# D of the RWKV inverse from the transposed E, and the GLA output's products grouped by shape

## The reference

```python
# RWKV-7, per token (8 heads of 64)
S = S * d - (S @ kk)[..., None] * (kk * a) + v[..., None] * k
y = S @ r
# GLA, per chunk of 32 tokens (4 heads, key 64, value 128)
att = where(causal, qe @ (k * exp(-b)).T, 0)
o = att @ v + qe @ S
S = S * exp(b_end) + (k * exp(b_end - b)).T @ v
```

## Time and profile before

| | before |
|---|---|
| median of 3 runs | 2339.72 us (2336.74 to 2341.12) |
| the profiled execution | 2343.12 us, its span 2341.3 us |
| PE busy | 2105.8 us, 90% of the span |
| DVE busy | 661.2 us, 28% |
| ACT busy | 343.9 us, 15% |
| mean granted PE clock | 0.929 of full speed |

### The profile page before, as it was taken

The page is one execution under the profiler, slowest core; times in us unless marked ns, Lnnn a source line. Parts: engine busy times, 40 slices in busy tenths (PEclk is TensorE's granted clock), DMA queues, the critical chain, the costliest instruction groups (busy, mean ns, idle before and its releaser), DMA issues. The chain is left out here.

```text
span 2341.3 us, 32274 instructions
## 1 busy us (share of the span) xinstructions
PE 2105.8 (90%) x13264; PEld 1857.5 (79%) x13264; DVE 661.2 (28%) x1039; ACT 343.9 (15%) x630; POOL 137.1 (6%) x153
## 2 busy tenths in 40 slices
PE   6988998589999999998998787779999999999577
PEld 5876997378888888876887466669999999999566
DVE  4377565721000000035412754410000000000053
ACT  1553111110000000011131110100111111011011
POOL 0001101412000000001002000010000000000100
PEclk9998999799999999999999668759999999999778
DMA  4211000029222222222222001047887777887510
GB/s 156 63 54 54 2 2 24 18 98 380 76 77 72 85 80 74 72 67 86 72 73 92 41 21 37 1 177 266 281 276 252 255 263 258 279 280 256 192 64 37
DMA packets 74177, 293.38 MB, mean 125 GB/s; under 512 B 8576, under 2 KB 9728, under 8 KB 72816
## 3 DMA queue, kind: packets, MB, share of 16 engines
q1 hardware_dynamic: 63504, 254.95, 32.3%
q0 software_dynamic: 8256, 29.64, 3.4%
q10 hardware_dynamic: 2336, 7.62, 1.0%
HBM read 254.87 MB, written 37.31 MB: 125 GB/s over the span
## 5 line engine op out<-in xcount | busy, mean ns | idle before, releaser
L193 PE MATMUL ps<-normed,ring 128*128 128x260 f32 (+1 forms) x3424 | 766.0, 386 | 16.7 <-DVE normed L236 16.7
L193 PEld LDWEIGHTS ps<-normed,ring 128*128 128x128 f32 (+1 forms) x3424 | 655.4, 192 | 124.2 <-issue 22.4
L2232 PE MATMUL ps<-proj,ring 128*128 128x144 f32 x3168 | 394.2, 288 | 6.5 <-DMA ring<-in_w_moe_gu 6.5
L2232 PEld LDWEIGHTS ps<-proj,ring 128*128 128x128 f32 x3168 | 392.2, 192 | 7.0 <-issue 6.9
L2248 PE MATMUL ps<-wide,ring 128*128 128x144 f32 x1584 | 202.8, 288 | 0.0
L2248 PEld LDWEIGHTS ps<-wide,ring 128*128 128x128 f32 x1584 | 196.0, 190 | 0.9
L193 PE MATMUL ps<-proj,ring 128*128 128x260 f32 x640 | 152.1, 400 | 19.0 <-PEq L935 8.5
L193 PEld LDWEIGHTS ps<-proj,ring 128*128 128x128 f32 x640 | 127.7, 200 | 41.5 <-issue 14.0
L193 PE MATMUL ps<-wide,ring 128*128 128x260 f32 x704 | 154.6, 383 | 0.9 <-DVE wide L1244 0.9
L193 PEld LDWEIGHTS ps<-wide,ring 128*128 128x128 f32 x704 | 134.0, 190 | 21.5 <-DVE wide L1244 1.3
L2296 DVE TENSOR_TENSOR wide<-temps,ps 128x144 f32<-128x144 f32 x99 | 30.2, 305 | 399.6 <-PE ps L2232 399.6
(11 more groups left out here) (458 smaller groups left out, 1756.8 us busy)
## 6 DMA issues: line engine op xcount, KB each, us to landing
ring<-in_w_moe_gu SPq DMA_DIRECT2D x198, 512.0 KB, 4.4
ring<-in_w_moe_dn SPq DMA_DIRECT2D x72, 704.0 KB, 5.7
ring<-in_w_gu SPq DMA_DIRECT2D x44, 512.0 KB, 3.5
ring<-in_w_in_cd SPq DMA_DIRECT2D x25, 512.0 KB, 3.5
ring<-in_w_in_ab SPq DMA_DIRECT2D x22, 512.0 KB, 3.5
ring<-in_w_dn SPq DMA_DIRECT2D x16, 704.0 KB, 4.0
ring<-in_w_ple SPq DMA_DIRECT2D x16, 640.0 KB, 3.9
x_slots<-zeros POOLq DMA_DIRECT2D x19, 512.0 KB, 21.1
```

Of the source, the lines that this page charges most:

```text
L193: mm = pe.matmul(dst[0:width, a:a + HALF], slab[:, k * width:(k + 1) * width], x[:, a:a + HALF], start=first and k == 0, stop=last and k = ...
L2232: mm = pe.matmul(hid_psum(m, s), slot(Q_MOE + 2 * m + s)[:, f * P:(f + 1) * P], XG[:, f * W:(f + 1) * W], start=f == 0, stop=f == KD - 1)
```

## The change

In the RWKV inverse the product L759 and DVE's `update_d` go. From the second level on, PE transposes the E that the level before has updated (four transpositions behind the G of each half, into `ps[1]`), and ACT copies them into D (`keep_d`); the products of G and D wait for that copy. ACT's copies for the next set are put in between. In the GLA output the four large products of a head come first, then the thirty small ones; the flags of accumulation are set to suit.

```diff
                     for l in range(5):
                         for cc in range(2):
+                            mats = range(4 * cc, 4 * cc + 4)
                             if l:
                                 w(pe, "ee_up", nth(s, l - 1, cc))
...
-                            for n in range(4 * cc, 4 * cc + 4):
+                            for n in mats:
                                 mm = pe.matmul(ps[0][:, n * P:(n + 1) * P], AL[:, n, :], EE[:, n, :], start=True, stop=True)
                             g["g_mm"].on(mm)
+                            if l:
+                                for n in mats:
+                                    mm = pe.transpose(ps[1][:, n * P:(n + 1) * P], EE[:, n, :], ident)
+                                g["d_mm"].on(mm)
...
                         for cc in range(2):
                             w(pe, "g_read", nth(s, l, cc))
+                            if l:
+                                w(pe, "d_read", 8 * s + 2 * l + cc - 1)
                             for n in range(4 * cc, 4 * cc + 4):
-                                if l < 4:
-                                    pe.matmul(ps[1][:, n * P:(n + 1) * P], GG[:, n, :], DD[:, n, :], start=True, stop=True)
                                 mm = pe.matmul(ps[2][:, n * P:(n + 1) * P], DD[:, n, :], GG[:, n, :], start=True, stop=True)
-                            g["eg_mm"].on(mm)
+                            g["ge_mm"].on(mm)
...
+                def keep_d(s, l, cc):
+                    n = slice(512 * cc, 512 * cc + 512)
+                    w(act, "d_mm", 8 * s + 2 * l + cc - 1)
+                    g["d_read"].on(act.activation(DDs[s % 2][:, 4 * cc:4 * cc + 4], pairs(ps[1][:, n]), ACT.Copy))
+
...
                 for s in range(4):
-                    if s < 3:
-                        keep_al(s + 1)
-                        keep_bk(s + 1)
-                        keep_v(s + 1)
+                    for l in range(5):
+                        for cc in range(2 if l else 0):
+                            keep_d(s, l, cc)
+                        if s < 3 and l in (0, 3, 4):
+                            (keep_al, keep_bk, keep_v)[(0, 3, 4).index(l)](s + 1)
...
-                def update_d(s, l, cc):
-                    n = slice(4 * cc, 4 * cc + 4)
-                    w(dve, "eg_mm", nth(s, l, cc))
-                    S(dve.tensor_tensor(DDs[s % 2][:, n], DDs[s % 2][:, n], pairs(ps[1][:, 512 * cc:512 * cc + 512]),
-                                        ALU.subtract))
...
                         masked_g(s, l, 0)
-                        if l:
-                            update_d(s, l - 1, 1)
                         masked_g(s, l, 1)
                         if l in (1, 2) and s < 3:
                             keep_am(s + 1, l - 1)
                         update_e(s, l, 0)
-                        if l < 4:
-                            update_d(s, l, 0)
                         update_e(s, l, 1)
...
+                    dst = bank(O_BANK[h])
                     for c in range(NC):
-                        dst = bank(O_BANK[h])
                         pe.matmul(dst[:, c * P:(c + 1) * P], VT[:, c, h, :], ATT(h)[:, c * P:(c + 1) * P],
-                                  start=True, stop=False)
-                        for s in range(4 * c, 4 * c + 4):
-                            for half in range(2 if s else 0):
-                                e = slice(64 * half, 64 * half + 64)
-                                mm = pe.matmul(dst[e, 32 * s:32 * s + 32], GS[r, t, s - 1, e], qt(t)[r, 32 * s:32 * s + 32],
-                                               start=False, stop=s % 4 == 3)
+                                  start=c == 0, stop=False, skip_group_check=True)
+                    for s in range(1, 16):
+                        for half in range(2):
+                            e = slice(64 * half, 64 * half + 64)
+                            mm = pe.matmul(dst[e, 32 * s:32 * s + 32], GS[r, t, s - 1, e], qt(t)[r, 32 * s:32 * s + 32],
+                                           start=False, stop=True, skip_group_check=True)
                     o_mm.on(mm)
```

More of the change, by code:

```diff
@@ L628, in build_program @@
         names = ("ab_mm", "al_read", "am_mm", "am_read", "bk_mm", "bk_read", "v_mm", "v_read", "d_ready", "e_mm",
-                 "e_read", "g_mm", "g_read", "eg_mm", "ee_up", "q_mm", "q_read", "p_mm", "p_read", "z_mm", "y_mm",
+                 "e_read", "g_mm", "g_read", "ge_mm", "ee_up", "d_mm", "d_read", "q_mm", "q_read", "p_mm", "p_read", "z_mm", "y_mm",
                  "y_read", "z_read")
@@ L867, in update_e @@
                     n = slice(4 * cc, 4 * cc + 4)
-                    w(dve, "eg_mm", nth(s, l, cc))
+                    w(dve, "ge_mm", nth(s, l, cc))
                     S(dve.tensor_tensor(EEs[s % 2][:, n], EEs[s % 2][:, n], pairs(ps[2][:, 512 * cc:512 * cc + 512]),
                                         ALU.subtract), g["ee_up"])
-                def update_d(s, l, cc):
-                    n = slice(4 * cc, 4 * cc + 4)
-                    w(dve, "eg_mm", nth(s, l, cc))
-                    S(dve.tensor_tensor(DDs[s % 2][:, n], DDs[s % 2][:, n], pairs(ps[1][:, 512 * cc:512 * cc + 512]),
-                                        ALU.subtract))
                 dve.wait_ge(loaded.sem, loaded.count)
```

## The result

Median of 4 runs 2322.30 us (2320.43 to 2323.46) against 2340.11 (2336.74 to 2341.12) of the kernel before: ratio 0.9925, 95% interval 0.9913 to 0.9937. The forecast was 2321.4. The profiled execution took 2321.96, its span 2320.1; the mean granted clock was 0.931 (before 0.929), PE busy 2084.1 us, DVE 639.8, ACT 362.9.

The account below looks back on a forecast made before the run. PE was taken to bound the kernel (busy 90% of the span). RWKV -13.6 (-14.8 - 3.4 + 4.6) and GLA -4.7 make -18.3 us, from a median of 2339.72 to 2321.4 us, range 2314 to 2330.

Parts of the forecast that it names:

- -14.8 for products out and transpositions in: RWKV inverse, PE's queue: 256 product instructions (28.7 us) go and 128 transpositions (13.9 us) come, net -14.8 us.
- -3.4 for the wait in the middle of G: RWKV levels: 0.21 us lost between G's halves, waiting for `update_e`, goes in 16 levels, -3.4 us.
- four transpositions (0.44) stand in that place and cover it: Middle of G in each RWKV level: 0.44 us of transpositions would hide the second half's wait for `update_e`.
- +4.6 for the waits ahead of G: RWKV levels: G's start newly waits for the first `update_e`, ten times 0.23 and six times 0.39, +4.6 us.
- D at nothing: RWKV products' wait for ACT's copy of D: costed at nothing, tightest in the last set (ready 0.82, needed 0.90).
- RWKV in all: Whole RWKV inverse: -14.8 - 3.4 + 4.6 = -13.6 us, bounds -9 to -18.2.
- GLA, -4.7 taken, bounds 0 to -5.9: GLA output: fewer shape changes save 4.7 us; 0 if the clock stays low, at most 5.9 by DVE's end.
- the fourth head: Last head of the GLA output: 1.2 us saved if the slow clock stays, 3.0 if wholly in the fast stretch.
- The clock's loss of the whole GLA gain: Rival, GLA output: sum and last heads run at half speed, gain 0 instead of 4.7, 2326.1 us; chance 0.12.
- D late: Rival, RWKV levels: D's copy ends after `masked_g`, each of 16 levels loses 0.5, 2329.4 us; chance 0.08.
- the levels are not PE's: Rival, RWKV levels: the round of E, G, mask, product and subtraction sets the pace; 2335.0 us; chance 0.04.
- The inverse at half the clock: Rival, RWKV inverse: clock falls to 1.2 GHz, some +4.7 us a level, all sixteen +75, 2396 us; chance 0.03.

Follow-up runs that it names:

- t_twice: The changed kernel with every transposition of E issued twice; one run, 2337.69 us.
- transp_behind: The changed kernel with a level's eight transpositions behind both halves of G, not four behind each half; 2322.44 us, ratio 0.9931 against the kernel before.
- between_behind: The changed kernel with the next set's products and `keep_am` moved as in `prep_between` and the transpositions as in `transp_behind`; one run, 2328.78 us.
- prep_between: The changed kernel with the next set's products between the halves of the remaining product, and `keep_am` between those of `update_e`; 2317.87 us, ratio 0.9902 against the kernel before.
- d_twice: The changed kernel with ACT making each copy of D twice, one after the other; one run, 2321.05 us.

## Why the prediction was right, and where it was not

**-14.8 for products out and transpositions in: right.** The counts are 256 out and 128 in, the steps 0.112 and 0.109, no loss at the change between them, and `t_twice` measured a transposition at 0.109 in place.

**-3.4 for the wait in the middle of G: the amount was right, the reason wrong.** The failed step is "four transpositions (0.44) stand in that place and cover it". `transp_behind` has none there and still no wait there in any of the sixteen levels. G's two halves and `update_e`'s two halves form one ring per level. In these levels PE was late at one place of it: when it waits at G's start for the first half of E, the second half is ready 0.7 later (0.9 in levels without `keep_am`), and PE comes to it 0.99 later at the earliest. Counting -3.4 and +4.6 as two terms gave the right sum since one wait replaced another, which was luck; as a reason it would have led astray, and did in the expectation of `transp_behind`. `between_behind` shows the condition under which the transpositions are the cover: G's first half must be free.

**+4.6 for the waits ahead of G: right.** 0.23 and 0.39 were forecast, 0.22 and 0.40 came. For a set with `keep_am` the three terms make -4 x 0.92 - 0.84 + 1.24 = -3.28; the second and third sets measured 41.05 - 37.76 = 3.29. `prep_between` removes these waits in three sets (3 x 1.24 = 3.7) and gets 3.61 of the block back.

**D at nothing: right in sum, and only by little.** In the first three sets the copy has at least 0.6 to spare (`d_twice`, whose products of G and D lose there what they lose in the changed kernel). In the last set the cover of 0.08 was used up by the handover: the products' second half loses 0.12 (0.05 and 0.07 in its first two steps), but E is then ready at G, whose start loses 0.10 instead of 0.22. One wait stands for the other again.

**RWKV in all:** -13.6 forecast, -13.76 in the traces, -13.0 in the medians of that part alone (by its interval -9.8 to -17.6). The closeness is partly luck: the first set gained 3.08 where its terms make 3.28, the last 4.1 where they make 3.6. Most of the 0.5 there is a wait that the prediction did not count. In the last level of the last set of the kernel before, the second half of the product had to wait for its mask, which stood behind `update_d` in DVE's list:

```profile
382.74 0.69 DVE L875 TENSOR_TENSOR normed<-normed,ps 128x512 f32<-128x512 f32 x1
382.86 1.06 PE L760 MATMUL ps<-temps,normed 128*128 128x128 f32 x8
383.46 0.69 DVE L863 TENSOR_TENSOR temps<-ps,phase 128x512 f32<-128x512 f32 x1
...
384.21 1.16 PE L760 MATMUL ps<-temps,normed 128*128 128x128 f32 x8 [0.29 <-DVE temps L863]
```

It lost 0.55 there (384.21 - 382.86 is 1.35, eight steps are 0.90, and the second step is slow by 0.10); in the changed kernel the same half loses 0.12. So taking work off DVE, which the prediction counted only for the wait in the middle of G, paid in this place too.

**GLA, -4.7 taken, bounds 0 to -5.9: -5.45 in the medians of that part alone (by its interval -2.6 to -7.0), -4.5 and -6.0 in two traces.** The heads were right (5.30; 5.35). Mis-sized was the fourth head, taken at 1.2 with 3.0 as the other end: in both traces it ran wholly at the full clock, 3.0 us instead of 6.0. That the whole change still came so near to the forecast is luck, since the medians show 17.8 of the 19.8 us that the two blocks gain in the traces. In the whole change PE's end moved by 6.7, and DVE's end capped the gain at 6.0, as the 5.9 had said. What remains is when the clock rises in the sum: 2.6 us into it in every trace with both parts, 5.9 in that of the GLA part alone, and why is open.

**Rivals.** The clock's loss of the whole GLA gain did not happen. D late costs in `between_behind` what the rival said (0.5 a level; 0.58), so its mechanism is real. One cover is enough to keep it away: the next set's products ahead of the product of G and D (`transp_behind`, first three sets), or four transpositions already in the middle of G (`prep_between`); `between_behind` has neither. That the levels are not PE's is ruled out by `t_twice`: 32 more steps of PE made a set longer by exactly their 3.49. The inverse at half the clock did not happen, nor in `t_twice`. The Trainium skill, "TensorE: Matmul & The Clock Gate", Part 4: PE-mode transpose, says that transpositions don't count as busy for the clock in the way products do; the trace disagrees, since the clock rose to 1.00 behind 4.6 us of transpositions alone. That it stays at 1.00 in `t_twice`, where a third of the work is transposition, fits but proves less, as two thirds are products.

## What to carry to other kernels

When a change takes a wait out of a ring of engines and puts one in, work out where in the ring the engine is late before the change and where after it, and name that place; a wait that goes may have gone because of the one that came, and not because of the cover that was meant for it. An operation costed at nothing beside a copy or a subtraction is worth a test with that cover doubled or taken away, since what hides it is often work of another step: with the preparation moved and the transpositions put together (`between_behind`), the wait for the copy of D came out in every level from the second on, at 0.58 each. And where the remaining wait is for a neighbour's result, look for work that can stand between the two halves: `prep_between` gave a quarter as much again in this block (3.61 on 13.76) for code that only changed its order.

## What the runs showed of the hardware

- A float32 transposition of 128x128 is one instruction with a step of 0.109 us, the float32 product of that shape two instructions of 0.112 each; changing between them costs nothing, while the step into the 64-row products of L684 is 0.20, and so is the step out of them, each with one of 0.21 behind it.
- PE starts 0.05 us after DVE's instruction ends (252.97 behind 252.92) but 0.14 after ACT's (355.94 behind 355.80). Behind a wait for DVE its second step is 0.21 instead of 0.11, also where the wait itself costs nothing: G at 356.91 starts one plain step of 0.112 after the product, and its second step is 0.21.
- In the GLA output, at a granted clock of 0.50, a change from 128x128 to 64x64 products and back costs some 0.44 us of PE ((6.67 - 5.35) / 3), at 1.00 some 0.31 ((3.79 - 2.85) / 3).
- In the GLA block the granted clock was 0.50 over 13.6 us in which PE was busy 13.26, and rose during the sum, at different points of it in different kernels.
